# Adding the experts' gated results onto the rows of x, doing the final norms inside the second projection, and choosing tokens in two halves

## The reference, cut to what matters

```
aff = softmax(hx @ router_w)                       # 1024 tokens x 16 experts
vals, idx = top_k(transpose(aff), 128)             # each expert takes its 128 best tokens
xs  = hx[idx]
hid = silu(xs @ w_gate[e]) * (xs @ w_up[e])
out = (hid @ w_down[e]) * vals[..., None]
x   = x + g2 * zeros.at[idx].add(out)              # scatter-add over the 16 experts
x   = rmsnorm(x, final_g)                          # end of the first block
hdn = rmsnorm_2(x, norm_gain_2)                    # second block
proj = hdn @ w_in_2                                # 1024 -> 3328 columns, 7 column blocks
q_a, k_a, v_a, g_a, q_b, k_b, v_b, g_b = split(proj)
...                                                # norms of q and k, rotation, attention, output
x = x + mixed @ w_out_2
```

## Time and profile before

| | |
|---|---|
| median of 3 runs | 2611.59 us (2610.48 to 2615.28) |
| the profiled execution's own time | 2614.48 us |
| its span, first to last instruction | 2612.7 us |
| mean granted TensorE clock | 0.933 |
| choice of tokens | 1112 to 1175 us of the span |
| experts' products | 1188 to 1763 us |
| combine, to the first product of the second projection | 1773.3 to 1872.0 us |
| second projection | 1872 to 2222 us |

### The profile page before, as it was taken

One profiled execution on the slowest core, in us unless ns is written; L12 is line 12 of the kernel. 1 busy time (PEld: TensorE's weight loads), 2 busy tenths in 40 slices (PEclk: granted clock), 3 DMA queues, 4 the chain that ended last, 5 costly groups with the idle time before them and its releaser, 6 DMA issues. The chain is left out here.

```text
span 2612.7 us, 50661 instructions
## 1 busy us (share of the span) xinstructions
PE 2172.6 (83%) x21068; PEld 1747.6 (67%) x21068; DVE 1714.1 (66%) x2582; ACT 1247.8 (48%) x2311; POOL 675.0 (26%) x469
## 2 busy tenths in 40 slices
PE   4899996799999878907999999991389999678989
PEld 2677785678888527706878888871277777456767
DVE  3665545888888454295999999975368475455642
ACT  3312221576666534316888888854322232454420
POOL 0000011666666102140322333304335443000000
PEclk9999998899999989958999999995599999899989
DMA  7222233233322374266999999966633431000042
GB/s 251 56 61 71 61 85 83 63 69 72 72 65 53 134 278 138 97 257 211 356 389 389 387 393 390 393 237 224 233 105 93 143 108 49 19 1 1 1 161 97
DMA packets 167311, 414.48 MB, mean 159 GB/s; under 512 B 13726, under 2 KB 57900, under 8 KB 167084
## 3 DMA queue, kind: packets, MB, share of 16 engines
q1 hardware_dynamic: 146572, 347.79, 38.1%
q0 software_dynamic: 11648, 42.47, 6.3%
q10 hardware_dynamic: 8864, 20.99, 2.1%
HBM read 356.15 MB, written 55.05 MB: 157 GB/s over the span
## 5 line engine op out<-in xcount | busy, mean ns | idle before, releaser
L1892 DVE TENSOR_TENSOR exp_w_lo<-exp_w,exp_w_hi 128x2048 fp32r<-128x2048 f32 x186 | 414.4, 2290 | 24.3 <-ACT exp_w_hi L1849 24.2
L1849 ACT ACTIVATE exp_w_hi<-exp_w 128x1024 fp32r<-128x1024 f32 x384 | 377.3, 1052 | 78.2 <-PE bank L1815 52.7
L2218 PE MATMUL bank<-w_hi,h_lo 128*128 128x512 f32 (+1 forms) x448 | 175.6, 392 | 34.1 <-DMA h_lo<-h_tiles 25.7
L2187 POOL TENSOR_TENSOR w_lo<-heads_a,w_hi 128x512 fp32r<-128x512 f32 (+1 forms) x104 | 138.3, 1355 | 185.4 <-ACT w_hi L2233 185.4
L2218 PE MATMUL bank<-w_hi,h_hi 128*128 128x512 f32 (+1 forms) x448 | 171.9, 384 | 0.0
L2218 PE MATMUL bank<-w_lo,h_hi 128*128 128x512 f32 (+1 forms) x448 | 171.8, 384 | 0.0
L1815 PE MATMUL bank<-exp_w_hi,xsT_lo 128*128 128x512 f32 x512 | 161.2, 396 | 6.5 <-DVE xsT_lo L1896 6.5
L1815 PE MATMUL bank<-exp_w_lo,xsT_hi 128*128 128x512 f32 x512 | 159.4, 393 | 0.0
L1815 PE MATMUL bank<-exp_w_hi,xsT_hi 128*128 128x512 f32 x512 | 159.4, 393 | 0.0
L1783 POOL DMA_INDIRECT moe_rows<-exp_out,idxT x16 | 25.2, 1575 | 439.4 <-DVE exp_out L1943 439.4
L1762 POOL DMA_INDIRECT xs<-xn_rows,idxT x16 | 115.9, 7242 | 37.3 <-DVE idxT L1914 28.5
(11 more groups left out here) (352 smaller groups left out, 5655.1 us busy)
## 6 DMA issues: line engine op xcount, KB each, us to landing
exp_w<-in_exp_w_gate_dram SPq DMA_DIRECT2D x64, 1024.0 KB, 10.2
exp_w<-in_exp_w_up_dram SPq DMA_DIRECT2D x64, 1024.0 KB, 10.6
exp_w<-in_exp_w_down_dram SPq DMA_DIRECT2D x64, 1024.0 KB, 7.4
heads_a<-in_w_in_dram SPq DMA_DIRECT2D x96, 256.0 KB, 2.7
ada_w_second<-in_ada_w_dram SPq DMA_DIRECT2D x16, 1024.0 KB, 7.1
chunk<-rkv_scratch SPq DMA_DIRECT2D x80, 192.0 KB, 4.0
w_in_ring<-in_w_in_dram SPq DMA_DIRECT2D x26, 512.0 KB, 4.0
rkv_scratch<-work POOLq DMA_DIRECT2D x16, 640.0 KB, 5.9
```

Of the source, the lines that this page charges most:

```text
L1849: last = act.activation(wh[:, n % RH, k, :], w[:, n % RING, k, :], ACT.Copy)
L1892: dve.tensor_tensor(wl[:, n % RH, :, :], w[:, n % RING, :, :], wh[:, n % RH, :, :], ALU.subtract).then_inc(lo_ok, 1)
L2187: pool.tensor_tensor(wl[:, q % SR, 0:width(q)], w[:, q % WR, 0:width(q)], wh[:, q % SR, 0:width(q)], ALU.subtract).then_inc(w_lo, 1)
L2218: mm = pe.matmul(g.ps[m % 4][:, 0:cols], lhs[:, t % HT, k, :], rhs[:, q % SR, 0:cols], start=(k == 0 and p == 0), stop=(k == KT - 1 and p ...
```

## The change

Four things are changed together.

1. **Tokens are chosen in halves.** `affT` becomes 48 partitions of 512: rows 0 to 15 hold the experts' affinities for the first 512 tokens, rows 32 to 47 those for the other 512 (rows 16 to 31 are filler). The same 16 rounds find the 128 best of each half at once. Then the two sorted lists are merged: the later half's list is reversed by a product with a flipped identity, and for each place i the greater of `first[i]` and `later[127-i]` is taken, which gives the 128 best of both.
2. **g2 is multiplied in where the expert's result leaves its bank**, by a `scalar_tensor_tensor` in place of a `tensor_scalar`, and the rows are added onto x itself: the x rows are stored into `moe_rows`, and the zeroing goes.
3. **`phase_combine` goes.** Both norms, the transposes and the splits are in `phase_second_project`: for the four tiles of the first half ahead of the weights' work, for the other four at m = 8, 10, 20 and 22. The second norm's gain is multiplied on the rows. Of a first-half tile the parts stay in SBUF; of a second-half tile they are stored to `h_tiles` and loaded when the second half begins.
4. **The second projection's details.** The weight ring has 4 pieces in place of 6, and POOL makes the low part of all pieces, the first 8 too.

```diff
-            dve.tensor_copy(g.affT[:, 0:512], g.ps[0][0:NE, :])
-            dve.tensor_copy(g.affT[:, 512:T], g.ps[1][0:NE, :])
+            dve.tensor_copy(g.affT[0:SECOND, :], g.ps[1][0:SECOND, :])
+            step(dve.tensor_copy(g.affT[SECOND:SECOND + NE, :], g.ps[1][SECOND:SECOND + NE, :]))
+            dve.tensor_copy(g.affT[0:NE, :], g.ps[0][0:NE, :])
...
-            for t in range(TT):
-                pool.dma_start(moe_v[t], zero[:, :]).then_inc(zeroed, 16)
...
-            dve.tensor_copy(g.valsT[:, :], g.ps[7][:, 0:NE])
-            dve.tensor_copy(g.idxT[:, :], g.ps[7][:, NE:2 * NE]).then_inc(picked, 1)
+            dve.tensor_copy(halves[:, 1], turned[:, :, SECOND:SECOND + NE]).then_inc(later, 1)
+            step(dve.tensor_copy(halves[:, 0], turned[:, :, 0:NE]))
+            dve.wait_ge(flipped, 1)
+            dve.tensor_tensor(taken[:, :], halves[:, 0, 0], value, ALU.is_ge)
+            step(dve.scalar_tensor_tensor(offset[:, :], halves[:, 0, 1], -float(T // 2), index, ALU.add, ALU.subtract))
+            dve.tensor_tensor(g.valsT[:, :], halves[:, 0, 0], value, ALU.max)
+            step(dve.tensor_tensor(offset[:, :], offset[:, :], taken[:, :], ALU.mult))
+            step(dve.scalar_tensor_tensor(offset[:, :], index, float(T // 2), offset[:, :], ALU.add, ALU.add))
+            dve.tensor_copy(g.idxT[:, :], offset[:, :]).then_inc(picked, 1)
...
-                        last = dve.tensor_scalar(o[:, e % 2, s], g.ps[6 + q][:, :], g.valsT[:, e:e + 1], None, ALU.mult)
+                        last = dve.scalar_tensor_tensor(o[:, e % 2, s], g.ps[6 + q][:, :], g.valsT[:, e:e + 1], g.g2[:, s], ALU.mult, ALU.mult)
...
-    WR, SR = 6, 14
+    WR, SR = 4, 14
+    AT = {HT: 2 * HT, HT + 1: 2 * HT + 2, HT + 2: 5 * HT, HT + 3: 5 * HT + 2}
+    LATER = {m: t for t, m in AT.items()}
...
 # tensor
+            turn_rows(0)
             for m, (n, t) in enumerate(tiles):
-                if n == 0:
-                    pe.wait_ge(h_in[t % HT], 32 * (t // HT + 1))
+                if m < HT:
+                    pe.wait_ge(h_lo, t + 1)
+                    if t + 1 < HT:
+                        turn_rows(t + 1)
+                elif n == 0:
+                    pe.wait_ge(h_in[t % HT], 32)
...
                 if m >= 2 and tiles[m - 2] in rot_no:
                     turn(rot_no[tiles[m - 2]])
+                if m - 1 in LATER:
+                    turn_rows(LATER[m - 1])
...
 # scalar
+            for i in range(HT + 2):
+                if i < HT:
+                    root(i, 0)
+                if 1 <= i < HT + 1:
+                    root(i - 1, 1)
+                if i < 4:
+                    split(2 * i)
+                    split(2 * i + 1)
+                if i >= 2:
+                    high(i - 2)
...
+                if m - 2 in LATER:
+                    high(LATER[m - 2])
+                if m in LATER:
+                    root(LATER[m], 0)
+                    root(LATER[m], 1)
...
 # vector
-            for q in range(KT):
-                dve.wait_ge(w_hi, q + 1)
-                dve.tensor_tensor(wl[:, q, :], w[:, q % WR, :], wh[:, q, :], ALU.subtract).then_inc(w_lo, 1)
+            dve.wait_ge(rows_in, 32)
+            for i in range(HT + 2):
+                if i < HT:
+                    final_norm(i)
+                if 1 <= i < HT + 1:
+                    second_norm(i - 1)
+                if i >= 2:
+                    low(i - 2)
...
+                if m - 2 in LATER:
+                    low(LATER[m - 2])
+                if m in LATER:
+                    final_norm(LATER[m])
+                    second_norm(LATER[m])
```

285 lines of the change are left out of this document (118 added, 167 removed).

## The result

The changed kernel takes 2543.15 us (median of 4 runs, 2540.3 to 2545.41), the kernel before, run beside it, 2613.44 us (2610.48 to 2619.82). The ratio is 0.9727, with a 95% interval of 0.9705 to 0.9749. The forecast was 2537, in a range of 2516 to 2560. The profiled execution took 2544.33 us, its span is 2542.6 us, against 2614.48 and 2612.7 before; so 70.1 us went, and the working had -74.5.

The account below looks back on a forecast made before the run. TensorE bounds the experts and projection; two stretches without products, 63 and 99 us, offered the gain. Terms -23.0 - 75.0 - 3.5 + 27 = -74.5 gave 2540.0 for the profiled execution, median forecast 2537 us, range 2516 to 2560 (own range 2524 to 2548).

Parts of the forecast that it names:

- Part 1: Choice of tokens: halved rounds save 25.6 us, a third copy costs 0.65 and the merge 1.9, together -23.0 us.
- Rival D: Choice of tokens: the 16 rounds stay at 3.88 us and the merge is added, 2563 us; chance 0.04.
- Part 2: Experts' results: multiplying g2 in at the bank and dropping the zeroing changes nothing on the path, 0 us.
- rival E: Experts' stage: VectorE's passes with a second input go as slowly as the worst row, 2557 us; chance 0.01.
- Part 3: Last scatter to rotation: VectorE starts m = 0 at T+42, -75.0 us; its waits for products go, -3.5 us.
- Rival B: Start of the projection: slower first tiles, so that m = 0 starts on VectorE at T+57, 2552 us; chance 0.14.
- The -3.5: Projection: with TensorE two tiles ahead, VectorE no longer waits for its products and its turn, -3.5 us.
- Part 4: Later tiles 4 to 7 in the projection: TensorE waits for their root and norm chains, at half clock after stops, +27 us.
- the four stops: TensorE's stops for tiles 4 to 7 in the projection; under 15 or over 40 us in sum would refute the prediction.
- the +2 of the working: Projection: tile 5's low part in the full blocks of VectorE (m = 12) costs +2 us.
- Rival A: Projection: the later tiles are hidden, only their transposes show, 4 us; 2514 us; chance 0.09.
- C: Projection: the later tiles cost double, 27 becomes 50 us, since a late weight piece stops TensorE again; 2560 us; chance 0.09.

Follow-up runs that it names:

- halves_alone: The kernel before with only the choice of tokens in halves and the merge; combine, zeroing and projection as before: 2591.41 us, ratio 0.991.
- spare_squares: The changed kernel with ScalarE writing the squares of tiles 0 to 3 into a scratch of their own, not the normed rows' buffer: 2537.35 us, ratio 0.9707.
- no_later_norms: The changed kernel without the roots, norms and transposes of tiles 4 to 7; their copies, loads and stores stay: 2529.14 us, ratio 0.9678.
- turns_only: The changed kernel without the roots and norms of tiles 4 to 7; their transposes, copies, loads and stores stay: 2526.67 us, ratio 0.9659.

## Why the prediction was right, step by step

**Part 1, -23.0: right.** The rounds saved 25.4 us (25.6 predicted). The difference of 512 elements in a subtraction, 0.534 us, held for all three passes: MAX8 went from 1.22 to 0.69, FIND_INDEX8 from 1.21 to 0.68, MATCH_REPLACE8 from 1.20 to 0.67. The cast to the gather grew by 1.2 us instead of 1.9. halves_alone shows the part alone: -24.4 us in the median. Rival D, that the rounds do not halve, is out. Ahead of the rounds the profile had +4.9, where the working had 0.65 for the third copy; the fourteen profiles show it as scatter. The 4.3 us between the profiled sum (2540.0 forecast, 2544.33 measured) are as much as this; the other terms missed by up to 3.4 us each and cancel.

**Part 2, 0: right.** The result with a second input took 744 ns, 746 before. The row that reads a bank was the right one, and rival E, built on the row with two SBUF inputs beside POOL, is out. The -1.6 us of the stretch is less than the 582.5 to 587.8 over which it scatters.

**Part 3, -75.0 and -3.5: the first right, the second right by luck in part.** Measured -73.0 and -5.4. T was to be 0.7 us later behind the experts than before; it is 11.5 us behind the last result, against 11.4 before, which takes 0.6 off. The start of VectorE came at T+44.5 instead of T+42, the first product at T+26.3 instead of T+23. Two things were missed in following tile 0. Its second norm started later and took 2.34 us beside a POOL pass (+1.7 by its end). And ScalarE stands still for 3.73 us, because the squares of tile 2 overwrite the rows of tile 0: a wait on a reused buffer which stands in the diff (`act.wait_ge(turned, t - 1)`) and has no row in the old trace. spare_squares took it away: the first product moved by 2.6 us and m = 0 by 3.5, from T+44.5 to T+41.0 (1789.26, T = 1748.30). Rival B (T+57) is out: ScalarE and VectorE do release each other four times a tile, but the tiles overlap.

The -3.5 stood for VectorE no longer waiting for products and for its turn in the first tiles. That gave 2.2 us, in the first three tiles. The other 3.2 of the 5.4 come from POOL being idle beside VectorE's last steps of tile 7, which the working did not have; TensorE gains nothing by them (39.3 becomes 37.1 at product 8), and they come off the gate block's column. That -73.0 and -5.4 add up to the forecast -78.5 within 0.1 is chance.

The lock between VectorE and GpSimd that the Trainium skill states (SBUF — State Buffer, Who interferes with whom) is met here too: the norm is 1.28 us where POOL is idle and 2.34, 2.39 and 2.10 where it works. The trace agrees with the rule. The working allowed 1 us on each of the first three passes; in the changed kernel they took 1.28, 1.62 and 2.34 us, 1.4 more than alone in all. The lock came back as the reason why spare_squares kept only part of its gain, and its largest price was one that the working did not have: the step of 5.08 us in the full block.

**Part 4, +27: right in mechanism, the terms too large.** Cut at VectorE, m = 8 to m = 28 grew by 25.8 us: +14.1 in the gate block (13.7 predicted for tiles 4 and 5), -0.1 in the full block (+2 predicted), +10.1 and +1.6 from m = 20 to 28 (11 for tiles 6 and 7). That agrees closely, but in part by the place of the cuts: the gate block's column holds the 3.2 us that the column before it gave up, and that from m = 20 holds 2.8 which tile 19 gave up, for the same reason. At TensorE's products it is +10.0, +3.6 and +8.6, 22.3 in all. So tiles 4 and 5 were put 3.7 too high and tiles 6 and 7 2.4 too high, and the full block 1.6 too low.

The mechanism is shown. Tile by tile the waits were 3.08, 3.42, 5.79 and 1.65 us, 13.9 in all, and no_later_norms and turns_only put 15.2 and 16.4 of the 22.3 us on the roots and norms: that is close to the 13.9 of waits and the 2.9 us by which the transposes took longer than at full clock (7.0 against 4 x 1.03). The prediction called itself wrong if the four stops added up to under 15 us. By the waits alone they do (13.9), with the slow transposes they do not (16.8); it had not said which it meant.

The 6 to 7 us that stay without any norm: 2.8 or 2.9 in the full block, where tile 5's low part and VectorE's step of 5.1 us beside four pieces stand (the +2 of the working had the low part alone); 1.1 and 1.7 in the gate block, with transposes at 0.8 us each in turns_only (1 us assumed); and 3.2 and 1.4 behind product 20, with waits of 3.10 and 1.11 us for tile 4's fetched part, which the working did not have. How much the bank copies or the ring of four add to this no run here isolates. Rival A (all of it hidden but the transposes) and C (double) are out.

Against the page's drain behind a table load, 1.38 us by the Trainium skill (ScalarE: Activation LUTs, What ACT_TABLE_LOAD costs), the new rows repeat the old ones: the load at 1842.65 takes 1.28 us and the root starts at 1843.94. No row shows the drain.

**The range and the chances** rested on the sum of four terms of known sign, of which the two large ones could be read from rows. Cut at VectorE none was off by more than 2 us in the profile, apart from the scatter; cut at TensorE the later tiles were put 4.7 us too high and the start's second term 1.3 too large. The 4.7 make up for the +4.9 ahead of the rounds, so the 6.2 us by which the median lies above the forecast are less than the single errors, by luck.

## What to carry to other kernels

Where a stage handles all tiles before the next engine starts, follow one tile through it: what decides is when the engine that bounds the next stage gets its first tile. Work that moves into an in-order engine's stream should stand at least one chain length behind the work that feeds it (here two tiles for a chain of 10 us), in a stretch where the bounding engine has room, and never behind a buffer or bank that the tile before it still holds. In following a tile, go through the diff for waits on reused buffers too, for the old trace has no row for them. And when stretches are compared, cut them at the engine that bounds them: a cut at another engine moved 3 us from one column into the next here and made a term look exact that was not.

## What the runs showed of the hardware

- MAX8, FIND_INDEX8 and MATCH_REPLACE8 over 48 x 512 take 0.69, 0.68 and 0.67 us, over 16 x 1024 MAX8 takes 1.22: time went by elements per partition, at about 1.04 ns each ((1.22 - 0.69) / 512), and three times the partitions did not lengthen it.
- Waits of TensorE of 3.08, 3.42 and 5.79 us each had eight transposes at 1.97 us behind them, half clock; after one of 1.65 us they took 1.10. Without a wait they took 1.03 to 1.04.
- Beside POOL's subtractions VectorE's instructions with SBUF operands alone are stretched: a copy of 128x128 took 1.35 us instead of 0.23, and a product of 128x512 5.08 us beside four subtractions in a row (5.02 us) instead of 0.69. The copy's neighbours took 1.22 and 1.32 us, each about one subtraction of POOL (1.3 us); the product lasted as long as four.
- Executions of this kernel differ by up to 12 us before the same instruction (first MAX8 at 1110.3 to 1122.2) while the 39.7 us from there to the gather repeat within 0.1. An edit of a few microseconds is better read from its own stretch than from the time of the run.
